# A second starting address for the last tiles of the split activations in a transformer kernel

## What is computed

```python
x = x + merged @ w_mix_out                                  # first model, mixing
x = x + cross_attention(rms_norm(x), rms_norm(mem), w_cq, w_ckv, w_co)
x = x + conv_ffn(rms_norm(x), w_ffn_in, ..., w_ffn_out)     # 1024 -> 2 x 2816 -> 1024
x = rms_norm(x)
for l in range(2):                                          # second model
    x = x + 0.5 * rms_norm(swiglu(rms_norm(x), ffn1_w13[l], ffn1_w2[l]))
    x = x + rms_norm(token_mixing(rms_norm(x), w_in[l], ..., w_out[l]))
    x = x + rms_norm(cross_attention_2(rms_norm(x), rms_norm(mem), ...))
    x = x + 0.5 * rms_norm(swiglu(rms_norm(x), ffn2_w13[l], ffn2_w2[l]))
return x
```

## Time and profile before

| What | Value |
|---|---|
| Time, median of 3 runs | 2020.77 us (2020.24 to 2022.79) |
| The profiled execution, its own time | 2029.09 us |
| Its span | 2026.9 us |
| PE (matmul) busy | 1993.8 us, 98% of the span, 14968 instructions |
| PEld (weight load) busy | 1842.6 us, 91% |
| DVE, ACT busy | 1345.3 us (66%), 1083.3 us (53%) |
| DMA queue of the weights | 356.90 MB, 51.6% of 16 engines' span |

### The profile page before, as it was taken

The page is one execution under the profiler, slowest core; times in us unless marked ns, Lnnn a source line. Parts: engine busy times, 40 slices in busy tenths (PEclk is TensorE's granted clock), DMA queues, the critical chain, the costliest instruction groups (busy, mean ns, idle before and its releaser), DMA issues.

```text
span 2026.9 us, 36882 instructions
## 1 busy us (share of the span) xinstructions
PE 1993.8 (98%) x14968; PEld 1842.6 (91%) x14968; DVE 1345.3 (66%) x1876; ACT 1083.3 (53%) x1708; POOL 51.8 (3%) x47
## 2 busy tenths in 40 slices
PE   7999999999999999999999999999999999999998
PEld 7989988999899989899998998999899989887887
DVE  6776766777476657866867555655477677756554
ACT  5845555554454454555556444644464555646443
POOL 0021000000000000000100000000000001000000
PEclk9999999999999999999999999999999999999999
DMA  7422454655566647533553655555555535545553
GB/s 278 171 75 75 143 189 159 203 193 193 173 218 198 196 167 231 183 136 129 205 202 136 214 190 194 195 192 186 197 197 188 175 114 187 176 164 179 180 187 123
DMA packets 98726, 359.25 MB, mean 177 GB/s; under 512 B 11192, under 2 KB 11512, under 8 KB 98296
## 3 DMA queue, kind: packets, MB, share of 16 engines
q1 hardware_dynamic: 98560, 356.90, 51.6%
HBM read 353.65 MB, written 1.05 MB: 175 GB/s over the span
## 4 chain that ended last, share of the span: by engine, by line
PE 93%; DVE 3%; ACT 2%; issue 1%; DMA 0%; SPq 0%; DVEq 0%; ACTq 0%
PE ps L1045 16%; PE ps L1047 15%; PE ps L1046 15%; PE ps L1032 8%; PE ps L1121 7%; PE ps L1119 7%; PE ps L1120 7%; PE ps L1201 2%; PE ps L1232 2%; PE ps L1234 2%; PE ps L1233 2%; PE ps L1088 2%; PE ps L1086 2%; PE ps L1087 2%; PE ps L1202 2%; PE ps L1208 2%
## 5 line engine op out<-in xcount | busy, mean ns | idle before, releaser
L1731 DVE TENSOR_TENSOR wlo<-raw,whi 128x1024 fp32r<-128x1024 f32 x635 | 773.8, 1228 | 453.3 <-ACT whi L2475 451.4
L2475 ACT ACTIVATE whi<-raw 128x1024 fp32r<-128x1024 f32 x635 | 664.9, 1056 | 366.5 <-PE ps L1121 153.5
L1045 PE MATMUL ps<-H,whi 128*128 128x256 f32 x2288 | 648.4, 283 | 2.2 <-DVE wlo L1731 2.0
L1047 PE MATMUL ps<-H,wlo 128*128 128x256 f32 x2288 | 639.2, 279 | 0.0
L1046 PE MATMUL ps<-L,whi 128*128 128x256 f32 x2288 | 638.7, 279 | 0.0
L1045 PEld LDWEIGHTS ps<-H,whi 128*128 128x128 f32 x2288 | 431.1, 188 | 7.9 <-issue 4.2
L1047 PEld LDWEIGHTS ps<-H,wlo 128*128 128x128 f32 x2288 | 431.5, 189 | 0.0
L1046 PEld LDWEIGHTS ps<-L,whi 128*128 128x128 f32 x2288 | 430.9, 188 | 0.6
L1119 PE MATMUL ps<-whi,HH 128*128 128x512 f32 x440 | 171.3, 389 | 0.0
L1121 PE MATMUL ps<-wlo,HH 128*128 128x512 f32 x440 | 171.2, 389 | 0.0
L1120 PE MATMUL ps<-whi,HL 128*128 128x512 f32 x440 | 171.2, 389 | 0.0
(11 more groups left out here) (439 smaller groups left out, 3169.5 us busy)
## 6 DMA issues: line engine op xcount, KB each, us to landing
raw<-in_ws SPq DMA_DIRECT2D x635, 512.0 KB, 3.4
prow<-in_rows SPq DMA_DIRECT2D x11, 512.0 KB, 5.2
row<-in_rows SPq DMA_DIRECT2D x9, 512.0 KB, 6.1
mema<-in_memT SPq DMA_DIRECT2D x4, 512.0 KB, 4.8
mema<-in_mem2T SPq DMA_DIRECT2D x4, 512.0 KB, 6.3
memb<-in_mem2T SPq DMA_DIRECT2D x4, 512.0 KB, 5.6
DT<-in_dec SPq DMA_DIRECT2D x2, 768.0 KB, 6.6
X<-in_x SPq DMA_DIRECT2D x1, 1024.0 KB, 10.5
```

What stands on the lines that cost most here:

```text
L1045: e.matmul(o, h, hs[k], start=first and k == 0, stop=False, skip_group_check=True)
L1047: mm = e.matmul(o, lo, hs[k], start=False, stop=last and end, skip_group_check=True)
L1731: e.tensor_tensor(m.wlo[:, n % SPL, :], r, h.bitcast(F32), SUB).then_inc(*c.lo.done(n))
L2475: e.activation(m.whi[:, n % SPL, :], m.raw[:, n % RAW, :], ACT.Copy).then_inc(*c.hi.done(n))
```

## The change

`BEGIN[s]` now holds for H and for L a triple (first, place, rest). Tiles below `first` begin at byte `place` and the others at byte `rest`, through the new class `Tiles`, which hands an index to one of two views of the same store. Where an instruction writes tiles on both sides of `first`, the new `stretches` cuts it in two; only `jh` does so. In it ACT cuts where H's `first` falls, and DVE where H's or L's does.

| Stage | Tiles of H at 96 | Tiles of L at 96 |
|---|---|---|
| x0, c, f | 7 | 7 |
| ("a", 0) | none | 7 |
| ("m", 0) | 4 to 7 | 4 to 7 |
| ("c", 0), ("b", 0) | 6, 7 | 6, 7 |
| ("a", 1) | 7 | none |
| ("m", 1) | 5 to 7 | 5 to 7 |
| ("c", 1) | 4 to 7 | 4 to 7 |
| "mix", ("o", l), ("b", 1) | none | none |

```diff
-BEGIN = {"x0": (64, 64), "mix": (0, 0), "c": (64, 64), "f": (64, 64), ("a", 0): (64, 64), ("m", 0): (64, 64), ("o", 0): (0, 0), ("c", 0): (64, 64), ("b", 0): (64, 64), ("a", 1): (64, 64), ("m", 1): (64, 64), ("o", 1): (0, 0), ("c", 1): (64, 64), ("b", 1): (0, 0)}
+BEGIN = {"x0": ((7, 64, 96), (7, 64, 96)), "mix": ((0, 0, 0), (0, 0, 0)), "c": ((7, 64, 96), (7, 64, 96)), "f": ((7, 64, 96), (7, 64, 96)), ("a", 0): ((0, 64, 64), (7, 64, 96)), ("m", 0): ((4, 64, 96), (4, 64, 96)), ("o", 0): ((0, 0, 0), (0, 0, 0)), ("c", 0): ((6, 64, 96), (6, 64, 96)), ("b", 0): ((6, 64, 96), (6, 64, 96)), ("a", 1): ((7, 64, 96), (0, 64, 64)), ("m", 1): ((5, 64, 96), (5, 64, 96)), ("o", 1): ((0, 0, 0), (0, 0, 0)), ("c", 1): ((4, 64, 96), (4, 64, 96)), ("b", 1): ((0, 0, 0), (0, 0, 0))}
...
+class Tiles:
+
+
+    def __init__(self, store, first, place, rest):
+        self.first, self.end = first, 8
+        self.lead, self.body = (store[:, at // 4:at // 4 + 8 * T].rearrange("p (k t) -> p k t", k=8) for at in (place, rest))
+
+    def __getitem__(self, at):
+        k = at[1].start if isinstance(at[1], slice) else at[1]
+        return (self.lead if k < self.first else self.body)[at]
+
+
+def stretches(begin, end, *tiles):
+
+    cuts = sorted({begin, end} | {t.first for t in tiles if begin < t.first < end})
+    return [slice(a, b) for a, b in zip(cuts, cuts[1:])]
...
     def high(self, s):
 
-        return self.begun(self.H_store, 8, BEGIN[s][0])
+        return Tiles(self.H_store, *BEGIN[s][0])
 
     def low(self, s):
 
-        return self.begun(self.L_store, 8, BEGIN[s][1])
+        return Tiles(self.L_store, *BEGIN[s][1])
...
-        at = slice(4 * j, 4 * j + 4), slice(128 * tb, 128 * tb + 128)
-        tt(m.low(s)[:, at[0], at[1]], four(bank), m.high(s)[:, at[0], at[1]].bitcast(F32), SUB, ("L", s, tb, j))
+        t = slice(128 * tb, 128 * tb + 128)
+        for k in stretches(4 * j, 4 * j + 4, m.high(s), m.low(s)):
+            tt(m.low(s)[:, k, t], four(bank)[:, k.start - 4 * j:k.stop - 4 * j, :], m.high(s)[:, k, t].bitcast(F32), SUB, ("L", s, tb, j))
...
-        do(m.high(s)[:, 4 * j:4 * j + 4, 128 * tb:128 * tb + 128], four(banks.of("tx", s, tb, j)), ACT.Copy, ("h", s, tb, j))
+        t = slice(128 * tb, 128 * tb + 128)
+        for k in stretches(4 * j, 4 * j + 4, m.high(s)):
+            do(m.high(s)[:, k, t], four(banks.of("tx", s, tb, j))[:, k.start - 4 * j:k.stop - 4 * j, :], ACT.Copy, ("h", s, tb, j))
```

## The result

| | Kernel before | Changed kernel |
|---|---|---|
| Median of the timed runs | 2020.77 us (2020.24 to 2022.79) | 2037.92 us (2034.34 to 2039.26) |
| Ratio, 95% interval | | 1.0065 [1.004, 1.009] |
| The profiled execution, its own time | 2029.09 us | 2034.34 us |
| Its span | 2026.9 us | 2032.2 us |
| Matmuls in 100 us of f, ("a", 0), ("b", 0), ("a", 1) | 851, 885, 851, 851 | 849, 850, 847, 853 |

The forecast was 2006.5 us, faster. The kernel became slower, as rival C had it. The medians of three are 17.2 us apart, 0.85%, more than the ratio says; why isn't shown.

A forecast was written before the change was run, and what follows sets the result against it. PE, busy 98%, was taken as the bound, through start-to-start matmul spacing and any new idle time. From 2020.8 us, -14.1 - 4.3 + 3.8 + 0.3 = -14.3 gave 2006.5 us, range 1996.5 to 2026.

The forecast's parts named there:

- rival C: The jump throws fast matmul streams out and slow ones stay; 2028.9 us, up to 2036.6; chance 0.14.
- The two cadences: Equal 256-wide matmul streams on PE run steadily at either 113.3 or 117.8 ns, 4.44 ns (3.9%) apart.
- four fifths of slow streams: Of 3600 matmuls outside the four feed-forward stages, 2900 taken as slow, worth 12.9 us at most.
- part (1): Moving last tiles by 32 bytes puts 1734 of 7824 matmuls at 96, disturbing the cadence; the fast one, once met, holds.
- part (2): Slow streams turn fast: -14.1 us in f, ("b", 0) and ("a", 1), -4.3 us (one third of 12.9) elsewhere.
- The cadences repeat from run to run: Three timed runs within 2.6 us taken to show that streams keep their cadence rather than drawing it each time.
- The price of 96: The 1734 matmuls reading tiles at 96 cost 0 to 7.7 us over the fast cadence; +3.8 us taken.
- The cut copies: Copies in `jh` cut in two: 14 more instructions on ACT, 16 on DVE, 2.5 us each; +0.3 us taken.
- the cover: Before ("a", 1), 4.5 us on ACT and 3.1 on DVE to spare before PE reads, against 0.18 and 0.34 added.
- A: The address has no say, the restart alone selects the cadence; no change, some 2021 us; chance 0.14.
- B: Only some streams move, one feed-forward stage in three and little else; -5 us, 2015.8 us; chance 0.20.
- slip of the clock: TensorE's clock partly at 1.2 GHz in two recurrence stretches; another timing may add or remove about 2 us.

The follow-up runs named there:

- all112: Changed kernel with all tiles of H and L at 112 in the stages that had 64; 2006.07 us, ratio 0.9912; once more 2006.46 us, 0.9903.
- jump64: Changed kernel with tiles 0 to 6 at 64 and tile 7 at 128 in every stage that moves; 2031.83 us, ratio 1.0034.
- change_again: Changed kernel as it was, run once more with a second profile; 2038.55 us against 2022.78 for the kernel before, ratio 1.0071.
- again: Kernel before, unchanged, beside itself with a second profile; 2030.66 us against 2029.59, ratio 1.0004.
- splits_only: Changed kernel with every tile back at 64 and the copies still cut in two; 2025.01 us, ratio 0.9977.
- all96: Changed kernel with every tile at 96 in the stages that had 64, no jump and no cut copy; 2049.05 us, ratio 1.009.
- cut4: Changed kernel with tiles 0 to 3 at 64 and 4 to 7 at 96, no copy cut; 2041.11 us, ratio 1.0055.
- starts_c: Changed kernel with one uniform start per stage, 112 and neighbours from 104 to 120, and 48; one run, 2044.64 us beside 2022.78.
- starts_a: Changed kernel with another uniform start for H and L in each of ten stages, 0 to 224; one run, 2033.79 us beside 2024.07.
- around112: Changed kernel with tiles at 112, tile 7 jumping in three feed-forward stages to 144, 128 or 176, and ("a", 0) at 240; 2016.47 us beside 2027.61.

## Why the prediction was wrong

**The two cadences: right.** They are 113.3 and 117.8 ns, and 4.7 us for a feed-forward stage; all112 lies where the forecast had put the kernel (2006.1 and 2006.5), because all its streams are at 113.3; that the two numbers meet so closely is chance, since the forecast counted on a third of the other streams and a price for 96. Its four fifths of slow streams outside the feed-forward stages were right: in before their steps under 130 ns lie 12.9 us over 113.3 ns each.

**The step that failed** is in part (1): "I take it that such a jump disturbs the phase that holds a stream in its cadence, and that the fast one, once met, holds." The first half is right. The second has it the wrong way round at a start of 64: there 117.8 ns is what survives the jump. Five feed-forward stages at 113.3 were seen to lose it at tile 7 (two in jump64, two in change_again, one in the changed kernel); none at 117.8 was seen to leave that for good. The -14.1 and -4.3 us of part (2) therefore never came. There was no row for the choice: the earlier trace rows show two cadences at 64, each undisturbed. Which of them comes back after a disturbance they can't show. The rows that could have warned were the restarts, which are disturbances too: the earlier trace rows have four streams in five at 117.8, and I used that only as an argument for rival C. Nor did the jump have to throw out every fast stream for the gain to fail: most stages were drawn slow from the head on, and the jump moved none of them.

**"The cadences repeat from run to run": wrong.** It was read out of three runs within 2.6 us. Runs again and splits_only show the draw in the profile, and the kernel before spreads over 15 us, by the draw and by the clock. Kernels in which no draw is seen spread less: all96 2.1 us, cut4 3.7, all112 3.4 and 0.6, the changed kernel 4.9 and 4.7; but the clock of all96, cut4 and all112 varied less too (by 0.002 at most, against 0.005). Here lies the size of the loss, as far as is known. The profile of before had one feed-forward stage at 113.3, and with it lost 7.2 us from c on. The three timed runs lie lower than its execution by 8.3 us. Up to some 4 us of that may be slips of the clock in x0 that they didn't have; their clock isn't known. The rest would be one more stage at 113.3, and without any help of the clock nearly two. So there was more to lose. All this is inferred from the times and not seen, since only the profiled execution has a trace.

**The price of 96 (+3.8 us of 0 to 7.7): the size was right, the footing not.** It is 2.2 ns over 117.8, 1734 x 2.2 = 3.8 us, on top of the long cadence and not on top of the short one. ("b", 0), with two tiles in eight, has 118.33 ns, and 117.78 + 2.2/4 is 118.33. Where H and L don't jump together the price is another one: ("a", 1), with H alone at 96, stays at 117.8 and pays nothing, and ("a", 0), with L alone, has 118.0 as f has with both.

**The sum as it came out.** Were all 7824 at 113.3 in all112 and at 117.8 plus the price in the change, that would be 7824 x 4.44 + 3.8 = 38.5 us between the two; measured are 31.8 (2037.9 and 2006.1), or 32.5 with the 2038.55 of change_again, whose runs stood beside those of all112. The steps in the two traces close the sum, all that lie under 130 ns: those of the changed kernel are 35.9 us over 113.3 ns each and not 38.5, since some of its streams ran at 113.3 up to tile 7 and since nearly 200 steps next to a wait aren't among them; those of all112 are 3.6 us over it, which are its steps behind restarts. The difference is 32.3.

**The cut copies: right.** The shapes of the changed kernel on ACT and DVE, beside the earlier trace rows:

```profile
L2498 ACT ACTIVATE H<-ps 128x512 fp32r<-128x512 f32 x30 | 17.3, 592 | 32.4 <-PE ps L1179 32.3
...
L2498 ACT ACTIVATE H<-ps 128x384 fp32r<-128x384 f32 x10 | 4.9, 487 | 0.1
...
L2498 ACT ACTIVATE H<-ps 128x128 fp32r<-128x128 f32 x10 | 2.8, 278 | 0.0
```

487 + 278 - 592 = 173 ns where 175 were worked out; on DVE 548 + 280 - 685 = 143 where it was 158. PE's waits for ACT's H and DVE's L are 2.7 and 1.7 us as before, so the cover held, and cut4 and splits_only show it from either side.

**The rivals.** C was what happened, and the measured 2037.9 lies 1.3 us above its 2028.9 to 2036.6. It counted on 1755 matmuls to lose, read from one execution, while the median of 2020.8 it started from probably had more of them. A and B gave an answer to 64 against 96 that no run bears out: the address has its say, and no stream was moved to 113.3. The Trainium skill's rule of the prediction ("SBUF — State Buffer", "Specifications (TRN2)": full bandwidth as long as at least two accesses fall on a line of 16 bytes) goes with A. It says nothing of the moving operand's place against the weights; 96 and 112 are both multiples of 16, and differ here by 6.7 ns in 113.3. The measurement decides.

**What stays open.** Why a cadence belongs to the addresses isn't shown. The addresses of the weights and of PSUM, the order of the three matmuls and the weight load under each may enter; only those of H and L were moved. Whether the 512-wide matmuls with H stationary gain at another start stays open too: they hold 87 in 20 us in the changed kernel as in the earlier trace rows, and their spacing is 233.3 ns at 64 and at 112, 234.2 at 96, 226.7 at 0. The prediction's slip of the clock was right, and its size, about 2 us, was low: the slips in x0 cost the changed kernel up to 3.9 us, and the first profile had none. What makes the clock fall in one execution and not in another stays open.

## What to carry to other kernels

Where nothing but matmuls fills a stretch, count them per 100 us: a difference of a few per cent between equal stages at a full clock is a cadence, not a wait, and here no engine's row named its cause. Read the granted clock of each stage before two spans are compared: here slips of the clock made a stage that had lost time, x0, look 2.2 us shorter. Before a disturbance is counted as a gain, ask which cadence the stream comes back to; one run with the start moved, and a second profile of the unchanged kernel, would have answered it here. And where a cadence is drawn per execution, three runs that agree say little: choose a start that leaves nothing to draw (here 112 for all tiles, 0.9% faster than before and the same within 3.4 us each time), and much of the spread goes with the time.

## What the runs showed of the hardware

The spacing of 128x256 fp32r matmuls behind one another at the full clock depends here on the byte at which H and L begin, with the weights at multiples of 512 bytes. From the stage that was given the start, by the trace's own start times:

| Start of H and L | Spacing, ns | Run |
|---|---|---|
| 112 | 113.3, after up to 15 steps | all112, starts_c |
| 64 | 113.3 or 117.8, drawn at a restart | before, again, splits_only |
| 16 | 116.7 over 167 matmuls and 118.7 over 118 (x0) | starts_a |
| 32 | 116.7 | starts_a |
| 240 | 117.1 | around112 |
| 192 | 117.8 | starts_a |
| 160 | 117.4 (head) to 118.9 (short stage) | starts_a |
| 48, 224 | 118.3, 118.4 (short stages) | starts_a, starts_c |
| 128 | 118.7 | starts_a |
| 80 | 118.3 (head), 119.0 over the mixer | starts_a |
| 0, 96, 108 | 120.0 | starts_a, all96, starts_c |
| 104 | 120.0, and 130.0 in one head | starts_c |
| 120, 116 | 120.8 (mixer: to 122.1), 121.7 | starts_c |

Not expected were three things: that a steady stream can have two spacings at one start and keep either for 1055 matmuls; that 4 bytes make the step from 120.0 to 113.3 ns; and that starts with the same remainder by 64 or by 128 differ (0, 64, 128 and 192; 112 and 240). All starts but 64, 96 and 112 rest on one execution, and 16 and 104 show a second spacing even there, so others may have been missed.
